# pw2 begins with eight outputs per tile, LayerNorm all on VectorE, and the borders of the stages rewritten

## The chip, the cores and the metric

The kernel runs on all 8 cores of one Trainium2 chip. The metric is device time in microseconds of the slowest core, as the median of several executions. The cores share no data: each works through the whole two-layer network for its own 1024 frames of the prompt (with 160 frames of history in front) and for two of the sixteen short sample sequences of 16 frames. So a microsecond that leaves the longest chain of one core leaves the time.

## The reference, cut to what matters

Everything is kept transposed, with channels on the 128 partitions (2048 channels are 16 chunks, called c or n) and frames along the free axis. Layer 0 mixes with a convolution module and layer 1 with sliding-window attention; each is followed by a SwiGLU. D is 2048, D_FF 5632.

```python
def conv_module(h, state, ...):
    a, gt = split(h @ w_pw1 + b_pw1, 2)
    u = a * sigmoid(gt)
    z = depthwise_conv(concat(state, u), width 31) + b_dw
    z = silu(layer_norm(z, ln_g, ln_b))        # per frame, over 2048 channels
    return z @ w_pw2 + b_pw2, last 30 frames of u

h = modulate(rms_norm(x, norm_mix), sh1, sc1)  # both layers
x = x + g1 * mixer(h)                          # conv_module, then attention
h = modulate(rms_norm(x, norm_ffn), sh2, sc2)
x = x + g2 * ((silu(h @ w_g) * (h @ w_u)) @ w_down)
...
y = rms_norm(x, norm_out)
```

Results are the normalized frames, the last 30 inputs of the convolution, and the keys and values of the newest 128 frames. All products run in bf16 with fp32 accumulation.

## The kernel before, in words

A core's columns stand in three tiles: columns 0 to 383, 384 to 767 and 768 to 1183 (widths 384, 384, 416; in layer 1 from wo on the first is 256 wide). The last tile holds 32 sample columns, whose modulation has another scale, so its evictions come in three pieces. Every engine's program is written out by hand: a helper `wait` puts semaphore waits ahead of the next instruction, and nothing is reordered afterwards. `mm` (line 229) issues every matmul, `act` (line 232) every ScalarE instruction and `dma` (line 224) every transfer, which is why most rows carry these three lines.

**Weights** go through RING, nine slots of 2048 columns. A block of 16 chunks takes two slots, a block of 8 takes one. `ring_use` makes TensorE wait for a block, `ring_release` marks it free once TensorE has finished, and `ring_fill` then issues the next loads in the fixed order of `plan`, on GpSimd's queue. A load can be issued only when the blocks that lie in its slots have been released.

**From the convolution to pw2.** `shift_copies` lays four shifted copies of a chunk of u, with 16 VectorE copies; `conv_tile` runs the depthwise convolution as small matmuls, ScalarE evicts z and its square, and VectorE adds both up in ACCZ and ACC2. `stat_sums` sums these over the partitions with fp32 matmuls, and `stat_factors` makes mean and 1/std of a tile. `ln_apply(t, c)` normalizes chunk c of tile t: subtract the mean (three chunks of four on GpSimd, one of four on VectorE, lines 928 and 931), multiply by 1/std (VectorE, line 933), silu on ScalarE into ZS; then SP reloads x into the place of z. pw2 has 16 output chunks. Six of them (three blocks of weights) are accumulated while the rows of a tile come, chunk by chunk in six banks, tile after tile. The six evictions of a tile (`epilogue_bias`: ScalarE into one of two buffers TMP2, then VectorE adds to x, line 456) stand behind the first rows of the next tile in ScalarE's program. The other ten outputs follow in `pw2_group`, one output of one tile at a time, in banks 3 to 6; block 3 is loaded while the six are at work, since three blocks hold six of the nine slots.

**Norms.** A `Norm` squares each finished output on ScalarE (four buffers), and TensorE adds the square to the sum of its tile in bank t; this add is put off by two groups of matmuls (`late`). When a tile has its sixteen adds, ScalarE makes 1/rms (Ln and Exp, another function table than Silu), and sixteen `scale` steps go to a list `behind`, which `after_group` empties by a credit of time: VectorE multiplies by 1/rms, ScalarE scales and shifts into HB. `samples` (lines 556 to 562) does the sample columns of the last tile and stands behind its sixteen rows. `need` empties the list up to the tile that TensorE is about to read. The last norm writes its result with `final`: four chunks on VectorE into one of two buffers, then a transfer to memory.

**SwiGLU.** For each of six groups G, `gate_up` makes the products of up to eight blocks and `down` adds their part of the output to x. The first two blocks of a layer are taken together, tile by tile, then the others one at a time. At the end of a stage `tile_outer` takes the last blocks together, so that the first tile is finished first: the last three blocks of pw2, of wo and of layer 0's `down`, and all eight of layer 1's `down`, each in the order of tiles 0, 1, 2.

**Attention** begins with `k_group` and `v_group`; the weights q_6 and q_7 are waited for before the first of them.

## Time and profile before

| | |
|---|---|
| median of 3 executions | 3349.31 us (3344.06 to 3625.43) |
| profiled execution | 3347.12 us |
| its span, slowest core | 3346.0 us |
| all cores' spans | 3325.3 to 3346.0 us |
| mean granted TensorE clock | 0.957 to 0.963 of full speed |
| TensorE busy | 3041.8 us, 91% of the span |
| VectorE / ScalarE / GpSimd busy | 1221.0 / 752.7 / 335.1 us |

The profiled execution's time is its span and 1.1 us around it. TensorE is the engine of the chain that ended last for 81% of the span, so the kernel's time is TensorE's work plus what TensorE waits and what it runs at the lower of its two clock levels (1.2 and 2.4 GHz; the granted clock is given as a share of the higher). The page cuts the span in 40 slices of 83.6 us:

```profile
PE   2399996889999999999999889898999999999996
...
PEclk8599997999999999999999999799999999999998
```

Both lines are full over most of the span. The slices that are not are the start, slices 7 to 9 (from 502 to 753 us: the end of the convolution, LayerNorm, pw2), the ones around 1840 to 1920 us (into attention), around 2090 to 2340 us (out of attention, wo, the next norm), and the last two.

### The profile page before, as it was taken

The numbers are of one execution on the slowest core, as the hardware profiler recorded it, in microseconds if no ns is written. First come the engines' busy times: TensorE is split into PE (matmuls) and PEld (weight loads), VectorE is DVE, ScalarE is ACT, GpSimd is POOL, SyncE is SP. The second block draws the span as 40 slices with busy tenths as digits, with TensorE's granted clock in tenths as the row PEclk, the third lists the DMA queues.
The fourth block names the chain that finished last, engine by engine and source line by source line (L and its number), as shares of the span: only waits on it lengthen the run. The fifth ranks groups of instructions, "written<-read, shape, count | busy, mean of one in ns | idle before, by whom it ended". The sixth has DMA issues, their size and how long they took to land.

```text
span 3346.0 us, 58403 instructions; the slowest of 8 cores (3325.3 to 3346.0 us)
## 1 busy us (share of the span) xinstructions
PE 3041.8 (91%) x23532; PEld 1857.9 (56%) x23566; DVE 1221.0 (36%) x2690; ACT 752.7 (22%) x1743; POOL 335.1 (10%) x510
## 2 busy tenths in 40 slices
PE   2399996889999999999999889898999999999996
PEld 0155553455556565565565555455566666666653
DVE  0356677331321414123413548723131313132315
ACT  1412224571000000000002647646100000000012
POOL 0000005000000000000001035410000000000000
PEclk8599997999999999999999999799999999999998
DMA  9977774525757475674667123032674444343432
GB/s 218 150 113 126 128 127 90 118 51 101 127 99 133 75 134 104 110 130 76 109 126 120 23 55 58 18 70 51 115 127 75 76 73 79 64 80 54 84 61 104
DMA packets 73592, 320.57 MB, mean 96 GB/s; under 512 B 11952, under 2 KB 28176, under 8 KB 45808
## 3 DMA queue, kind: packets, MB, share of 16 engines
q0 software_dynamic: 49440, 283.78, 48.9%
q1 hardware_dynamic: 23888, 33.06, 3.3%
q8 instruction: 192, 3.15, 0.4%
q14 instruction: 72, 0.59, 0.1%
HBM read 590.55 MB, written 10.70 MB: 180 GB/s over the span
## 4 chain that ended last, share of the span: by engine, by line
PE 81%; DVE 5%; ACT 5%; DMA 4%; issue 3%; another core or an unknown queue 1%; SPq 0%; DVEq 0%; ACTq 0%; POOL 0%; POOLq 0%
PE ps L229 80%; ACT SCR L232 2%; DMA RING<-wmod 2%; ACT HBraw L232 1%; DMA X<-xT 1%; PE ps L1349 1%; DVE X L933 1%; DMA RING<-wpw 1%; ACT RING L232 1%; DVE X L465 1%; DVE UBraw L578 1%; DVE UBraw L1355 1%; DVE X L456 0%; SPq L224 0%
## 5 line engine op out<-in xcount | busy, mean ns | idle before, releaser
L229 PE MATMUL ps<-HBraw,RING 128*128 128x384 bf16 (+4 forms) x10816 | 1762.4, 325 | 35.8 <-DVE HBraw L562 15.0
L229 PEld LDWEIGHTS ps<-HBraw,RING 128*128 128x128 bf16 x10848 | 1050.2, 98 | 716.1 <-issue 56.3
L229 PE MATMUL ps<-UBraw,RING 128*128 128x384 bf16 (+3 forms) x6016 | 968.9, 319 | 41.6 <-ACT SCR L232 22.1
L229 PEld LDWEIGHTS ps<-UBraw,RING 128*128 128x128 bf16 x6016 | 571.4, 99 | 403.9 <-issue 78.7
L620 DVE TENSOR_TENSOR UBraw<-ps,SCR 128x384 bf16<-128x384 f32 (+2 forms) x264 | 144.4, 547 | 1194.7 <-PE ps L229 1175.7
L232 ACT ACTIVATE SCR<-ps 128x384 f32<-128x384 f32 (+2 forms) x264 | 127.0, 481 | 1787.2 <-PE ps L229 1787.2
L465 DVE SCALAR_TENSOR_TENSOR X<-ps,MOD,X 128x384 f32<-128x384 f32 (+2 forms) x960 | 389.6, 447 | 319.9 <-PE ps L229 318.7
L224 POOL DMA_DIRECT2D RING<-wgu x88 | 46.5, 529 | 1094.6 <-PE ps L229 1091.1
L229 PE MATMUL ps<-SCT,RING 128*128 128x3 bf16 x3072 | 91.3, 165 | 64.3 <-DMA RING<-wmod 54.4
L224 POOL DMA_DIRECT2D RING<-wmod x96 | 51.5, 537 | 877.5 <-PE ps L229 869.1
L229 PEld LDWEIGHTS ps<-SCT,RING 128*128 128x128 bf16 x3072 | 89.8, 97 | 74.9 <-issue 66.8
L232 ACT ACTIVATE RING<-RING,NM 128x193 f32<-128x193 f32 (+1 forms) x264 | 116.7, 444 | 55.0 <-DVE NM L1317 54.9
L794 DVE COPY UBraw<-UBraw 32x1256 bf16<-32x1256 bf16 (+2 forms) x272 | 125.1, 460 | 5.1
L232 ACT ACTIVATE SCR<-X 128x384 bf16<-128x384 f32 (+3 forms) x160 | 88.0, 572 | 158.8 <-DVE X L465 68.3
L229 PE MATMUL ps<-SCR,ONESB 128*128 128x384 bf16 (+6 forms) x206 | 59.8, 349 | 69.5 <-ACT SCR L232 67.2
L229 PE MATMUL ps<-UBraw,SCR 128*32 128x384 bf16 (+4 forms) x2336 | 114.1, 295 | 5.1 <-DVE UBraw L794 3.0
L456 DVE TENSOR_TENSOR X<-X,SCR 128x384 f32<-128x384 f32 (+2 forms) x84 | 47.2, 562 | 180.7 <-ACT SCR L232 180.7
L232 ACT ACTIVATE HBraw<-SCR,MOD,AM 128x384 bf16<-128x384 f32 (+2 forms) x144 | 89.5, 689 | 44.0 <-DVE MOD L398 35.1
L224 POOL DMA_DIRECT2D RING<-wdn x96 | 50.9, 540 | 462.3 <-PE ps L229 462.0
L232 ACT ACTIVATE SCR<-ps,VTs 128x512 f32<-128x512 f32 (+5 forms) x116 | 63.4, 566 | 141.8 <-PE ps L229 141.6
L229 PEld LDWEIGHTS ps<-UBraw,SCR 128*32 128x32 bf16 (+2 forms) x2336 | 64.3, 98 | 48.3 <-issue 12.4
L767 DVE SCALAR_TENSOR_TENSOR UBraw<-ps,VTs,SCR 128x512 bf16<-128x512 f32 (+4 forms) x112 | 39.7, 402 | 115.6 <-ACT SCR L232 113.6
(95 smaller groups left out, 1235.3 us busy)
## 6 DMA issues: line engine op xcount, KB each, us to landing
RING<-wmod POOLq DMA_DIRECT2D x96, 1024.0 KB, 13.6
RING<-wgu POOLq DMA_DIRECT2D x88, 1024.0 KB, 8.9
RING<-wdn POOLq DMA_DIRECT2D x80, 512.0 KB, 8.2
RING<-wpw POOLq DMA_DIRECT2D x24, 1024.0 KB, 17.0
X<-xT SPq DMA_DIRECT2D x4, 2368.0 KB, 55.6
RING<-wqkv POOLq DMA_DIRECT2D x16, 512.0 KB, 6.5
X<-xT SPq DMA_DIRECT2D x32, 192.0 KB, 2.4
RING<-wo POOLq DMA_DIRECT2D x5, 1024.0 KB, 8.5
```

Of the source, the lines that this page charges most:

```text
L224: engw.e.dma_start(out=out, in_=in_).then_inc(sem, 16)
L229: return PE.emit(nc.tensor.matmul(out, lhsT=lhsT, rhs=rhs, start=start, stop=stop, **kw))
L232: return ACT.emit(nc.scalar.activation(out=out, in_=in_, func=func, **kw))
L456: DVE.emit(nc.vector.tensor_tensor(out=X[:, n, xlo:xlo + zn], in0=X[:, n, xlo:xlo + zn], in1=tmp[:, e, 0:zn], op=ALU.add))
L465: DVE.emit(nc.vector.scalar_tensor_tensor(out=X[:, n, a:b_], in0=PS[bk][:, a - xlo:b_ - xlo], scalar=MOD[:, li, 80 + n, bi:bi + 1], in1=X[ ...
L578: DVE.emit(nc.vector.scalar_tensor_tensor(out=YS[:, i, c % 4, 0:zn], in0=X[:, c, xlo:xlo + zn], scalar=VTs[:, VO["nout"] + c:VO["nout"] + ...
L620: DVE.emit(nc.vector.tensor_tensor(out=ACTR[:, 8 * (G % 2) + j - FIRST[G], xlo:xlo + zn], in0=bu[:, 0:zn], in1=SG[:, p, 0:zn], op=ALU.mult))
L767: DVE.emit(nc.vector.scalar_tensor_tensor(out=out, in0=ba[:, lo:hi], scalar=ba_s, in1=SGC[:, kk % 2, lo:hi], op0=ALU.add, op1=ALU.mult))
L794: DVE.emit(nc.vector.tensor_copy(out=U4[32 * s:32 * s + 32, cb, j, lo:hi], in_=U[32 * j:32 * j + 32, cb, 8 * s + lo:8 * s + hi]))
L933: DVE.emit(nc.vector.tensor_tensor(out=z, in0=z, in1=ACC2[:, zlo:zlo + zn], op=ALU.mult))
L1349: PE.emit(nc.tensor.transpose(PTB[0:hi - lo, c + 128 * u:c + 128 * u + 128], PB[i % 2][:, u, lo:hi], IDB[:]))
L1355: DVE.emit(nc.vector.tensor_copy(out=PTS[0:rows, i % 2, lo:hi], in_=PTB[0:rows, lo:hi]))
```

## The change: what it does

1. **LayerNorm.** `ln_apply` does the subtraction always on VectorE; GpSimd does none. `stat_sums(2)` and `stat_factors(2)` move behind the fourth row of tile 0, and the Ln and Exp of tile 2 (`stat_root`, split off) behind its sixteenth silu.
2. **pw2.** Four blocks are held. For each tile six outputs are accumulated as rows come and two more (n = 6, 7) behind them, from rows that are all there. The evictions of the six stand right behind them, in four buffers (TMP4), ahead of the next tile's rows; those of the two stand behind the fifth row of the next tile. Eight outputs are left for `pw2_group`.
3. **Last convolution chunk.** Four of sixteen shifting copies go to ScalarE, and the taps stand behind the copies.
4. **Norms.** Adds are put off by three groups instead of two; in pw2 and wo a square is issued one group later (`last`); every third `scale` step is done on VectorE alone; `samples` stands ahead of the sixteen rows of the last tile.
5. **SwiGLU.** The first three blocks of a layer are taken together instead of two, and the squares left over are flushed behind the first of their nine products. Layer 1's last `down` does block 0 for all tiles, then the seven others in the order of tiles 2, 1, 0.
6. **Attention.** q_6 and q_7 are waited for just ahead of their own products.

```diff
+        TMP4 = carve(SCR, 17152, (128, 4, 416), F32)
...
-                late.append((pe_groups[0] + 2, lambda: self.add(t, i, ta)))
+                late.append((pe_groups[0] + 3, lambda: self.add(t, i, ta)))
...
+                    if t == 2:
+                        behind.append((1.5, t, lambda: self.samples(tr)))
                     for c in range(KC):
                         behind.append((0.62, t, lambda c=c: self.scale(t, c, tr)))
-                    if t == 2:
-                        behind.append((1.5, t, lambda: self.samples(tr)))
...
-                ACT.wait(DVE.tick())
-                act(HB[:, c, 32 + xlo:32 + xlo + zn], self.tmp[:, i, 0:zn], AF.Identity, scale=AM[:, c, 0:1],
-                    bias=MOD[:, self.li, self.sh0 + c, 0:1])
-                self.tfree[i] = ACT.tick()
+                am, sh, row = AM[:, c, 0:1], MOD[:, self.li, self.sh0 + c, 0:1], HB[:, c, 32 + xlo:32 + xlo + zn]
+                if c % 3 == 2:
+                    DVE.wait(DVE.tick())
+                    DVE.emit(nc.vector.tensor_scalar(out=row, in0=self.tmp[:, i, 0:zn], scalar1=am, scalar2=sh,
+                                                     op0=ALU.mult, op1=ALU.add))
+                    self.tfree[i] = DVE.tick()
+                else:
+                    ACT.wait(DVE.tick())
+                    act(row, self.tmp[:, i, 0:zn], AF.Identity, scale=am, bias=sh)
...
                 if G == 0:
-                    two = [ring_use(f"gu{li}_{j}") for j in js[:2]]
+                    some = {}
                     for t in range(3):
-                        for j in (0, 1):
-                            gate_up(two[j][0], j, t, G)
+                        for j in js[:3]:
+                            if t == 0:
+                                some[j] = ring_use(f"gu{li}_{j}")
+                            gate_up(some[j][0], j, t, G)
+                            if t == 0 and j == js[0]:
+
+                                flush_late()
                             if t == 2:
-                                ring_release(two[j][1])
-                    js = js[2:]
+                                ring_release(some[j][1])
+                    js = js[3:]
                     flush_late()
...
-                inner = 5 if after.out else 0
+                inner = 5 if after.out else 1
                 for b in range(inner):
                     slot, bi = ring_use(f"dn{li}_{G}_{b}")
                     for n in (2 * b, 2 * b + 1):
                         for t in range(3):
                             down(slot, n, t, G)
                     ring_release(bi)
-                tile_outer([ring_use(f"dn{li}_{G}_{b}") + (2 * b,) for b in range(inner, 8)], tiles,
-                           lambda slot, n, t: down(slot, n, t, G))
+                tile_outer([ring_use(f"dn{li}_{G}_{b}") + (2 * b,) for b in range(inner, 8)],
+                           lambda slot, n, t: down(slot, n, t, G), (0, 1, 2) if after.out else (2, 1, 0))
             yield
 
...
+        def shift_copies(c, lo, hi, both=False):
+
             cb = c % 2
+            if both:
+                ACT.wait(DVE.tick(), conv_t[c - 2, 2])
             for j in range(4):
                 for s in range(4):
-                    DVE.emit(nc.vector.tensor_copy(out=U4[32 * s:32 * s + 32, cb, j, lo:hi],
-                                                   in_=U[32 * j:32 * j + 32, cb, 8 * s + lo:8 * s + hi]))
+                    out, in_ = U4[32 * s:32 * s + 32, cb, j, lo:hi], U[32 * j:32 * j + 32, cb, 8 * s + lo:8 * s + hi]
+                    if both and s == 3:
+                        act(out, in_, AF.Copy)
+                    else:
+                        DVE.emit(nc.vector.tensor_copy(out=out, in_=in_))
 
         def taps(c):
             DVE.emit(nc.vector.tensor_tensor(out=DG[:, c % 2, :, :], in0=M4[:].unsqueeze(1).to_broadcast([128, 32, 32]),
...
-            POOL.wait(rs_t[t])
             DVE.wait(rs_t[t])
-            if c % 4:
-                POOL.emit(nc.gpsimd.tensor_tensor(out=z, in0=z, in1=ACCZ[:, zlo:zlo + zn], op=ALU.subtract))
-                DVE.wait(POOL.tick())
-            else:
-                DVE.emit(nc.vector.tensor_tensor(out=z, in0=z, in1=ACCZ[:, zlo:zlo + zn], op=ALU.subtract))
-                DVE.wait(DVE.tick())
+            DVE.emit(nc.vector.tensor_tensor(out=z, in0=z, in1=ACCZ[:, zlo:zlo + zn], op=ALU.subtract))
+            DVE.wait(DVE.tick())
...
-        blocks = [ring_use(f"pw2_{b}") for b in range(3)]
-        waiting = []
-        pk = 2
-        for t, (zlo, zn) in enumerate(L0T):
-            now = [(pk + n) % 8 for n in range(6)]
-            pk += 6
-            for c in range(KC):
-                ln_apply(t, c)
-                if t == 0 and c == 3:
-                    stat_factors(2)
-                if c < len(waiting):
-                    ready.append((waiting[c][1], t - 1, pw2_out(*waiting[c])))
+            return n, t, epilogue_bias(0, n, zlo, zn, bk, tp, xr_t[t, n // 4], TMP4)
+
+
+
+        blocks = [ring_use(f"pw2_{b}") for b in range(4)]
+        six = (4, 5, 6, 7, 2, 3)
+
+        def pw2_mm(t, n, bk, c):
+            zlo, zn = L0T[t]
+            mm(PS[bk][:, 0:zn], blocks[n // 2][0][:, c, 128 * (n % 2):128 * (n % 2) + 128], ZS[:, c, zlo:zlo + zn],
+               c == 0, c == KC - 1)
+
+        for c in range(4):
+            ln_apply(0, c)
+        for t in range(3):
             for c in range(KC):
                 PE.wait(ap_t[t, c])
                 for n in range(6):
                     if c == 0:
-                        PE.wait(bfree[now[n]])
-                    mm(PS[now[n]][:, 0:zn], blocks[n // 2][0][:, c, 128 * (n % 2):128 * (n % 2) + 128],
-                       ZS[:, c, zlo:zlo + zn], c == 0, c == KC - 1)
-                    if c == KC - 1:
-                        now[n] = (t, n, now[n], PE.tick())
-            waiting = now
-        for slot, bi in blocks:
-            ring_release(bi)
-        for args in waiting:
-            ready.append((args[1], 2, pw2_out(*args)))
+                        PE.wait(bfree[six[n]])
+                    pw2_mm(t, n, six[n], c)
+                if t == 0 and c == 3:
+                    stat_sums(2)
+                    stat_factors(2)
+                    for c2 in range(4, KC):
+                        ln_apply(0, c2)
+                    stat_root(2)
+            tp = PE.tick()
+            for n in range(6):
+                ready.append(pw2_out(t, n, six[n], tp))
+            if t == 2:
+                for slot, bi in blocks[:3]:
+                    ring_release(bi)
+            two = []
+            for n in (6, 7):
+                PE.wait(bfree[n - 6])
+                for c in range(KC):
+                    pw2_mm(t, n, n - 6, c)
+                two.append((t, n, n - 6, PE.tick()))
+            if t < 2:
+                for c in range(5):
+                    ln_apply(t + 1, c)
+            for args in two:
+                ready.append(pw2_out(*args))
+            if t < 2:
+                for c in range(5, KC):
+                    ln_apply(t + 1, c)
+        ring_release(blocks[3][1])
...
-            norm1.square(n, t, pw2_out(t, n, bk, PE.tick()))
-            if ready:
-                norm1.square(*ready.popleft())
+            if last:
+                norm1.square(*last.popleft())
+            last.append(pw2_out(t, n, bk, PE.tick()))
+            for _ in range(2 if n < 10 else 1):
+                if ready:
+                    norm1.square(*ready.popleft())
             after_group(1.3)
...
-        q3 = [use_halves("q_6"), use_halves("q_7")]
+        q3 = []
...
+                if t == 0 and n % 2 == 0:
+                    q3.append(use_halves(f"q_{n // 2}"))
...
-            norm3.square(n, t, epilogue_bias(1, n, xlo, zn, bk, PE.tick()))
+            if last:
+                norm3.square(*last.popleft())
+            last.append((n, t, epilogue_bias(1, n, xlo, zn, bk, PE.tick())))
```

How the instructions stand now, at the three places that the prediction speaks of. First TensorE's program from the last convolution chunk into pw2, before the change (`UBraw,SCR` are convolution matmuls, `SCR,ONESF` the sums of `stat_sums`, `UBraw,RING` pw2, `SCR,ONESB` the adds of squares):

```order
L229 MATMUL ps<-UBraw,SCR 32x384 x32
L229 MATMUL ps<-UBraw,SCR 32x32 x32
L229 MATMUL ps<-SCR,ONESF 128x384 x2
L229 MATMUL ps<-SCR,ONESF 128x416 x2
L229 MATMUL ps<-UBraw,RING 128x384 x192
L229 MATMUL ps<-UBraw,RING 128x416 x96
L229 MATMUL ps<-UBraw,RING 128x384 x32
L229 MATMUL ps<-SCR,ONESB 128x384 x2
L229 MATMUL ps<-UBraw,RING 128x416 x16
L229 MATMUL ps<-SCR,ONESB 128x384 x2
L229 MATMUL ps<-UBraw,RING 128x384 x16
```

And in the changed program:

```order
L230 MATMUL ps<-UBraw,SCR 32x384 x32
L230 MATMUL ps<-UBraw,SCR 32x32 x32
L230 MATMUL ps<-SCR,ONESF 128x384 x2
L230 MATMUL ps<-UBraw,RING 128x384 x24
L230 MATMUL ps<-SCR,ONESF 128x416 x2
L230 MATMUL ps<-UBraw,RING 128x384 x232
L230 MATMUL ps<-UBraw,RING 128x416 x128
L230 MATMUL ps<-UBraw,RING 128x384 x32
L230 MATMUL ps<-SCR,ONESB 128x384
L230 MATMUL ps<-UBraw,RING 128x416 x16
L230 MATMUL ps<-SCR,ONESB 128x384 x3
```

The sums of tile 2 moved behind the first four rows of pw2 (24 matmuls), and 384 instead of 288 matmuls of pw2 stand ahead of the first add of a square.

ScalarE's program through the rows, before (`UBraw<-X,VTs` is a silu, `SCR<-ps,G1B,MOD` an eviction of pw2, the pair with `EPSC` the Ln and Exp of a tile):

```order
L232 ACTIVATE SCR<-SCR,EPSC 128x384
L232 ACTIVATE SCR<-SCR 128x384
L232 ACTIVATE UBraw<-X,VTs 128x384 x4
L232 ACTIVATE SCR<-SCR,EPSC 128x416
L232 ACTIVATE SCR<-SCR 128x416
L232 ACTIVATE UBraw<-X,VTs 128x384 x13
L232 ACTIVATE SCR<-ps,G1B,MOD 128x384
L232 ACTIVATE UBraw<-X,VTs 128x384
L232 ACTIVATE SCR<-ps,G1B,MOD 128x384
L232 ACTIVATE UBraw<-X,VTs 128x384
```

And in the changed program:

```order
L233 ACTIVATE SCR<-SCR,EPSC 128x384
L233 ACTIVATE SCR<-SCR 128x384
L233 ACTIVATE UBraw<-X,VTs 128x384 x16
L233 ACTIVATE SCR<-SCR,EPSC 128x416
L233 ACTIVATE SCR<-SCR 128x416
L233 ACTIVATE SCR<-ps,G1B,MOD 128x384 x6
L233 ACTIVATE UBraw<-X,VTs 128x384 x5
L233 ACTIVATE SCR<-ps,G1B,MOD 128x384 x2
L233 ACTIVATE UBraw<-X,VTs 128x384 x11
L233 ACTIVATE SCR<-ps,G1B,MOD 128x384 x6
L233 ACTIVATE UBraw<-X,VTs 128x416 x5
L233 ACTIVATE SCR<-ps,G1B,MOD 128x384 x2
```

The six evictions of a tile no longer alternate with silus of the next, and the Ln and Exp of tile 2 stand between tile 0's last silu and tile 0's evictions.

TensorE's program from the last pw2 groups into the SwiGLU of layer 0 (`HBraw,RING`), before:

```order
L229 MATMUL ps<-UBraw,RING 128x416 x16
L229 MATMUL ps<-SCR,ONESB 128x416
L229 MATMUL ps<-HBraw,RING 128x384 x32
L229 MATMUL ps<-SCR,ONESB 128x416
L229 MATMUL ps<-HBraw,RING 128x384 x96
L229 MATMUL ps<-HBraw,RING 128x416 x64
L229 MATMUL ps<-HBraw,RING 128x384 x64
L229 MATMUL ps<-HBraw,RING 128x416 x32
```

And in the changed program:

```order
L230 MATMUL ps<-UBraw,RING 128x416 x16
L230 MATMUL ps<-SCR,ONESB 128x416
L230 MATMUL ps<-HBraw,RING 128x384 x32
L230 MATMUL ps<-SCR,ONESB 128x416 x3
L230 MATMUL ps<-HBraw,RING 128x384 x160
L230 MATMUL ps<-HBraw,RING 128x416 x96
L230 MATMUL ps<-HBraw,RING 128x384 x64
L230 MATMUL ps<-HBraw,RING 128x416 x32
```

The left-over squares of tile 2 stand behind the first product, and five products (160 matmuls) instead of three stand between them and the first that reads tile 2 (128x416).

## Rows read from the trace of the kernel before

**Rows 1.** The page: its first line.

```profile
span 3346.0 us, 58403 instructions; the slowest of 8 cores (3325.3 to 3346.0 us)
```

**Rows 2.** Stretches: length, busy PE, PEld, DVE, ACT, POOL, clock, DMA share, GB/s.

```profile
538.00:630.00 92.00, 59.78 (x290) 29.39 (x288) 61.13 (x81) 51.81 (x85) 41.85 (x36) 0.82 0.39 109
630.00:793.00 163.00, 146.07 (x878) 82.35 (x879) 48.75 (x94) 87.04 (x163) 4.76 (x9) 0.95 0.35 64
1785.00:1925.00 140.00, 126.65 (x768) 74.42 (x767) 68.39 (x165) 70.81 (x130) 7.51 (x14) 0.98 0.34 56
2205.00:2377.00 172.00, 150.30 (x1189) 97.86 (x1188) 48.83 (x100) 87.55 (x179) 5.81 (x11) 0.97 0.39 71
3230.00:3331.00 101.00, 77.58 (x448) 43.45 (x446) 46.42 (x114) 28.65 (x56) 0.53 (x1) 0.94 0.18 58
```

**Rows 3.** Timeline of TensorE at the borders: start, length, instructions, idle before.

```profile
760.49 30.39 PE L229 MATMUL ps<-HBraw,RING 128*128 128x416 bf16 x160 [7.48 <-DVE HBraw L562]
...
1854.56 0.32 PE L229 MATMUL ps<-UBraw,ONESB 128*128 128x384 bf16 x1 [4.55 <-ACT UBraw L232]
...
1875.19 4.44 PE L229 MATMUL ps<-HBraw,RING 128*128 128x384 bf16 x16 [3.11 <-DMA RING<-wqkv]
...
2347.89 28.58 PE L229 MATMUL ps<-HBraw,RING 128*128 128x416 bf16 x160 [7.47 <-DVE HBraw L562]
...
3238.40 3.24 PE L229 MATMUL ps<-UBraw,RING 128*128 128x256 bf16 x16 [5.68 <-DMA RING<-wdn]
```

**Rows 4.** The same view, VectorE and GpSimd, end of convolution and LayerNorm.

```profile
509.24 6.88 DVE L794 COPY UBraw<-UBraw 32x1000 bf16<-32x1000 bf16 x16
...
539.48 4.97 DVE L933 TENSOR_TENSOR X<-X,SCR 128x384 f32<-128x384 f32 x4
...
587.23 0.55 DVE L931 TENSOR_TENSOR X<-X,SCR 128x384 f32<-128x384 f32 x1
587.88 1.97 DVE L933 TENSOR_TENSOR X<-X,SCR 128x384 f32<-128x384 f32 x4
...
533.04 45.17 POOL L928 TENSOR_TENSOR X<-X,SCR 128x384 f32<-128x384 f32 x36 [13.45 <-ACT SCR L232]
626.05 1.63 POOL L224 DMA_DIRECT2D RING<-wpw  x3 [47.83 <-issue]
```

**Rows 5.** The same view, TensorE in pw2.

```profile
542.97 6.55 PE L229 MATMUL ps<-UBraw,RING 128*128 128x384 bf16 x24 [3.83 <-ACT UBraw L232]
...
580.14 18.15 PE L229 MATMUL ps<-UBraw,RING 128*128 128x384 bf16 x94 [3.21 <-ACT SCR L232]
...
630.06 6.98 PE L229 MATMUL ps<-UBraw,RING 128*128 128x384 bf16 x32 [5.91 <-ACT SCR L232]
...
640.34 2.76 PE L229 MATMUL ps<-UBraw,RING 128*128 128x384 bf16 x16
642.94 0.73 PE L229 MATMUL ps<-SCR,ONESB 128*128 128x416 bf16 x2
```

**Rows 6.** The same view, ScalarE in LayerNorm.

```profile
549.12 1.28 ACT L232 ACT_TABLE_LOAD   x1
550.42 2.50 ACT L232 ACTIVATE UBraw<-X,VTs 128x384 bf16<-128x384 f32 x4
...
568.27 0.65 ACT L232 ACTIVATE SCR<-ps,G1B,MOD 128x384 f32<-128x384 f32 x1
...
623.37 6.54 ACT L232 ACTIVATE SCR<-ps,G1B,MOD 128x384 f32<-128x384 f32 x18 [3.79 <-PE ps L229]
```

**Rows 7.** The loads of weights issued in 624:628, in the view of RING.

```profile
DMA to landing us min/median/max: 11.8/16.9/21.3
```

**Rows 8.** Stretches view of 2110:2150, in attention.

```profile
2110.00:2150.00 40.00, 27.38 (x217) 15.49 (x214) 30.23 (x51) 28.46 (x115) 21.08 (x26) 0.53 0.19 35
```

**Rows 9.** Timeline of VectorE at the end.

```profile
3330.98 4.59 DVE L578 SCALAR_TENSOR_TENSOR UBraw<-X,VTs,SCR 128x416 f32<-128x416 f32 x8 [2.69 <-ACT SCR L232]
3337.30 4.74 DVE L578 SCALAR_TENSOR_TENSOR UBraw<-X,VTs,SCR 128x416 f32<-128x416 f32 x8 [1.73 <-DMA yT<-UBraw]
```

More of the change, by code:

```diff
@@ L583, in final, with tile_outer @@
                                   YS[:, i, :, 0:zn], yst_sem[i])
-        def tile_outer(blocks, tiles, body):
-            for t in range(3):
+        def tile_outer(blocks, body, order=(0, 1, 2)):
+            for t in order:
                 for slot, bi, n0 in blocks:
@@ L740, in build_nc @@
         u4_t = {}
+        u4a_t = []
         conv_t = {}
@@ L903, in stat_factors @@
             rs_t[t] = ACT.tick()
-        PE.wait(u4_t[KC - 1])
+        PE.wait(u4_t[KC - 1], *u4a_t)
+        set_gb("bpw2", 0, 32)
         for b in range(2):
@@ L1444, in build_nc @@
         pk = 0
+        last = deque()
         def wo_group(rows, n, t):
@@ L1470, in build_nc @@
                 ring_release(i)
-        tile_outer([ring_use(f"wo_{b}") + (2 * b,) for b in (5, 6, 7)], L1T,
+        tile_outer([ring_use(f"wo_{b}") + (2 * b,) for b in (5, 6, 7)],
                    lambda slot, n, t: wo_group(whole(slot), n, t))
+        norm3.square(*last.popleft())
         DVE.wait(kv_t[0], kv_t[1])
```

39 lines of the change are left out of this document (21 added, 18 removed).

## The prediction

> **What bounds the kernel now.** I read the page first: TensorE is busy for 91% of a span of 3346.0 us [rows 1], so what can be won is TensorE's waits and its time at 1.2 GHz. The slices with low clock lie at borders of stages; the view of stretches gives each its size [rows 2]. From 538 to 630 us TensorE is busy 59.8 of 92.0 us at a granted clock of 0.82; in the four other stretches it idles 16.9, 13.4, 21.7 and 23.4 us (length minus busy). The timeline names the longest waits at these borders [rows 3]: for the sample columns of the last tile (7.48 and 7.47 us), for a burst on ScalarE when a tile's norm is made (4.55), for q_6 and q_7 (3.11) and for a block of `down` (5.68). After such a wait TensorE runs at the lower level: 16 matmuls of 384 columns take 4.44 us behind the wait of 3.11 [rows 3], where at 2.4 GHz they are 2.60 us from start to start (640.34 to 642.94) [rows 5], 0.1625 each; 416 columns are then 0.173.
>
> **LayerNorm and pw2 (changes 1 to 3).** On VectorE four multiplications take 1.97 us when GpSimd is silent, 0.49 each, and 4.97, 1.24 each, inside GpSimd's run of 45.17 us [rows 4]. Without GpSimd a row costs its subtraction, 0.65 from start to start (587.23 to 587.88), and 0.49: 1.14 us, or 1.20 at 416 columns. TensorE needs 6 x 0.1625 = 0.98 for it, so VectorE sets the pace.
>
> Start: 12 instead of 16 copies save 4 x 0.43 = 1.7 us [rows 4] and the shorter ones another 0.9 by their columns. No row shows the copies on ScalarE. Four of 1000 columns are at least 4 x 0.62 (a 384-column silu [rows 6]), at most 1000/384 times that, 2.5 to 6.5 us; VectorE's share (5.2, and about 1.2 for the taps) covers them, save for a few tenths at the top. I take 2.6 us for this, and 2.8 us for accumulation and factors that GpSimd no longer slows. The first row starts at 542.97 - 5.4 = 537.6.
>
> Tile 0: four rows as now, 6.5 us [rows 5]. Then comes a new wait: the moved sums (2.5 us, my estimate between 1.7 and 3.1), the factors on VectorE (2.0, three operations in sequence), one row (1.1) and its silu (0.7), and TensorE idles some 4 us before the fifth row at 550.5; it starts at 551.27 now. Eleven rows, the matmuls of the last and some slow ones give 564.5 for the six outputs. The pair behind needs 32 x 0.1625 = 5.2 us and covers part of the next interval.
>
> Intervals: six evictions at 0.65 on ScalarE [rows 6], the last addition 0.6, sixteen rows 18.2, the two evictions behind the fifth row 2.5 (VectorE waits for silus and evictions), last silu 0.7, its matmuls 1.0: 26.9 us; 28.1 at 416 columns. Between tiles 0 and 1 the Ln and Exp of tile 2 add 2.8, as each switch of table is 1.28 [rows 6]. So the six of tile 1 end at 594.2, of tile 2 at 622.3, the pair at 627.9. SP's reloads of x, one behind each silu, come closer together, but the evictions need rows 0 to 7 only, asked for 8 rows earlier: nothing. In the trace the table load of 549.12 is followed by a silu at 550.42 [rows 6], so a switch costs the load alone. The Trainium skill ("ScalarE: Activation LUTs", What ACT_TABLE_LOAD costs) gives 1283 ns plus a drain of about 1380 ns for each. By that the two switches would make the interval 2.8 us longer; the trace shows no such drain, and the sum leaves it out.
>
> Then the weights. The plan needs pw2_0's slots for pw2_4, and with four blocks held (eight of nine slots) nothing is loaded ahead. The release falls at 622.3. Of three loads issued together at 626.05 [rows 4] the first landed after 11.8 us, the others after 16.9 and 21.3 [rows 7]. I take 11.8, the same position in the same queue: TensorE waits until 634.1, 6.2 us, and loses 1.4 in the restart as at 630.06 now (6.98 for 32 [rows 5], 5.2 at full rate). With an idle memory it could be 9; with more in flight, 16.9, and both stay in the range. At 635.5, 24 of 48 output tiles are done. Now 18 are done at 630.06, and six more with their adds take 20.1 (3.1 each, 1.4 slow): 650.2. **Term A: 14.7 us.**
>
> **Into the SwiGLU (changes 4, 5).** From 630 to 793 us TensorE idles 16.9 and loses 4.7 at the low level (1.4 after a burst; 3.3 after 760.49, where 160 matmuls take 30.39 [rows 3] against about 27.1). Nine products stand at the head instead of six before another block, five instead of three ahead of tile 2, and the samples come first: the wait of 7.48 and its restart go. Putting adds off by one more group and one square later covers most of the bursts, but four square buffers bound it. A third of the rows goes to VectorE: 45 in three norms at 0.5 us, 22 us; it is busy 48.8 of 163 us here [rows 2], so they hide behind TensorE. No row shows this form; half of it or twice it hides too, unless several stand together. I leave 4.5 us of waits and 2 for adds that no longer fall in the first six groups. **Term B: 15.5 us** (8 to 19).
>
> **Into attention (4, 6).** 13.4 idle and 3.2 at the low level. The wait for q_7 moves behind the first products of k and v, by when it has landed; but the last rows of tile 0's norm were made behind it and are late next, about 1.5 us. I leave 7. **Term C: 9.5** (5 to 12).
>
> **wo into the SwiGLU (4, 5).** 21.7 idle, 3.4 slow after 2347.89; 2.5 of it is a barrier that stays, 5.5 I leave: **term D: 17** (11 to 20). The third block held was requested two groups of wo before the stage and is needed after two products, some 14 us later.
>
> **The end (5).** 23.4 idle and 4 slow. Block 0 gives 8.6 us of work while block 7 loads (5.68 of waiting goes). The last tile is 256 wide, so its `final` steps are shorter; now they are two runs of 4.59 and 4.74 us with a store between them [rows 9]. Of the idle time about 9 stays, the bursts; the tail behind the last matmul shrinks by some 3.5. **Term E: 22** (13 to 27).
>
> Sum: 14.7 + 15.5 + 9.5 + 17 + 22 = 78.7. The profiled execution took 3347.12; minus 78.7 it is 3268.4. The median of the runs stands 2.2 above the profiled execution, which gives 3270.6: **3271 us**, 2.3% less.
>
> **The rivals.**
>
> *Bursts stay.* The adds may be held by the four buffers whatever the delay, and evictions queue behind Ln, Exp and scaled rows as now. For it: waits up to 4.55 us [rows 3] are longer than one group of `down` (1.6). Against: the long waits for samples and loads do not depend on it. B, C, D and E lose about 5 each: 3291.
>
> *The low clock stays in pw2.* A row leaves TensorE 0.16 us idle in 1.14, and each tile begins with a wait. In attention the clock stood at 0.53 for 40 us with TensorE busy 27.4 of them [rows 8]. Against: at 1.2 GHz a row needs 1.95 us and TensorE would be busy without a gap; at 580.14, 94 matmuls took 18.15 us [rows 5], 2.9 over the full rate, so it had returned. If half of the 63 us of row work runs slow, 30 us are lost, part of it hidden: 3296. The Trainium skill ("TensorE: Matmul & The Clock Gate", A second HAM failure mode: psum-queue depth-cycling) tells of a kernel whose short idles between groups made the clock go back and forth. That is this rival's mechanism; no row here shows it for gaps of 0.16 us.
>
> *Slower than before.* The same clock, kept from the first row to the last of the nine products, 537 to 757 us. That is 63 (384 matmuls), 70 (24 outputs with 36 adds) and 48 (nine products), 181 us of work at full rate; each of it at 1.2 GHz costs as much again. It decides from 79 us of such work on, where the sum is used up; all of it gives 3271 + 181 = 3452. Against it: between 640 and 690 us the groups ran at 2.60 with adds between them.
>
> *It does less than it says*: LayerNorm waits for reloads of x or the queue of SP, and A is nothing: 3286.
>
> *More than the sum*: bursts vanish and the block lands early, 20 us: 3251.
>
> **How the numbers follow.** A measurement of this kernel can tell about 2% from no change, that is 3282 us. Forecast as summed: 0.55, with its own range 3256 to 3286, of which 0.49 under 3282. More: 0.10. Bursts stay: 0.15. Low clock in pw2: 0.10, half of it with other terms at their low ends. A is nothing: 0.07. Slower: 0.03. Faster by over 2% is then 0.59, same 0.38, slower 0.03. The lower end takes in the case with more, the upper all low ends together with a late block: 78.7 less 36: 3307. The range is 3248 to 3308.
>
> **What would show it.** On VectorE single multiplications near 0.5 us all through LayerNorm, and rows 1.14 apart; TensorE with four waits in pw2: behind the fourth row, 3 to 4 us after tile 0, about 1.4 after tile 1, and 6 for RING<-wpw. No wait for DVE HBraw (the samples), none for RING<-wqkv before the first k product, none for RING<-wdn at the end; the tail behind the last matmul near 14 us. I am wrong if pw2's matmuls keep taking 0.32 us, if the wait for pw2_4 passes 10 us, or if a product waits for the third block of a SwiGLU.

## The result, and the profile after

The changed kernel took 3302.99 us (median of four runs, 3299.62 to 3308.97). The ratio to the kernel before is 0.9871, with an interval of 0.9843 to 0.9900: 43 us less, and 32 us more than the 3271 forecast. (Some executions of every kernel, here and below, were disturbed; ratios and the times quoted leave them out, and where few were left the interval is wide.) The mean of the eight cores' spans, which one late core hardly moves, fell from 3335.9 us in the profiled execution to 3291.0, and stands between 3288.8 and 3292.2 in all four runs; some differences below are given in it too. The page is that of core 5, the slowest of the profiled execution:

```profile
span 3300.6 us, 58445 instructions; the slowest of 8 cores (3281.4 to 3300.6 us)
```

All rows that follow are of core 2 unless said otherwise, the core of [rows 1 to 9]; its span fell from 3346.0 to 3292.7, by 53.3 us. To see where they came from I took from the timelines of TensorE the start of each stage's first matmul, on all eight cores, and the time from one such start to the next. Each number is the median of eight cores, in us; the sum is without what lies ahead of pw2 and behind the last matmul. The last row adds up the medians above it; "last gate_up" is its last matmul. The last five columns are experiments of the next section: banks is number 1, halves 5, both 10, delay 2 is 11, old entries 3.

| from ... to | before | after | banks | halves | both | delay 2 | old entries |
|---|---|---|---|---|---|---|---|
| pw2 to first gate_up of SwiGLU 0 | 188.1 | 171.1 | 176.0 | 167.2 | 167.0 | 169.0 | 179.7 |
| to its first down | 146.8 | **159.8** | 149.0 | 142.7 | 141.5 | 141.4 | 150.0 |
| to the last group of down | 904.3 | 904.7 | 904.6 | 904.3 | 904.3 | 904.3 | 904.5 |
| to the first v product | 97.0 | 85.6 | 86.4 | 87.4 | 88.9 | 94.1 | 94.1 |
| attention | 307.0 | 307.8 | 307.0 | 308.2 | 308.8 | 308.4 | 305.2 |
| to first gate_up of SwiGLU 1 | 125.9 | 113.6 | 113.6 | 113.6 | 113.6 | 113.7 | 126.9 |
| to its first down | 136.5 | **148.5** | 145.0 | 135.1 | 132.0 | 130.2 | 135.9 |
| to the last gate_up | 776.9 | 776.8 | 776.9 | 776.8 | 776.9 | 776.8 | 776.9 |
| to the last matmul | 96.8 | 74.8 | 75.0 | 75.0 | 75.1 | 88.8 | 89.4 |
| sum | 2779.2 | 2742.7 | 2733.5 | 2710.3 | 2708.0 | 2726.8 | 2762.6 |

Three stages are 11 to 22 us shorter, pw2 is 17 shorter, and two have become longer: each SwiGLU's stretch up to its first down, by 13.0 and 12.0 us. What wo won (12.3) is gone within 20 us. The view of stretches (length, busy time of each engine with the number of instructions, granted clock, DMA's share, GB/s), for LayerNorm with pw2's first part, the rest of pw2, and the two bad stretches:

```profile
536.00:633.00 97.00, 77.72 (x395) 39.70 (x396) 62.88 (x119) 54.95 (x92) 2.12 (x4) 0.90 0.48 118
633.00:709.00 76.00, 73.06 (x427) 41.61 (x426) 21.78 (x42) 46.37 (x94) 1.59 (x3) 0.98 0.40 75
709.00:869.00 160.00, 140.93 (x1024) 83.41 (x1023) 39.50 (x86) 35.26 (x62) 9.57 (x19) 0.93 0.57 98
2279.00:2428.00 149.00, 128.06 (x1029) 84.59 (x1027) 37.40 (x84) 33.91 (x60) 9.83 (x19) 0.92 0.60 105
```

In the third and fourth TensorE is idle for 19.1 and 20.9 us. The timeline of TensorE says where (start, length, instruction, and in brackets the idle time and who ended it), at the head of SwiGLU 0 and of SwiGLU 1:

```profile
708.64 5.36 PE L230 MATMUL ps<-HBraw,RING 128*128 128x384 bf16 x32
713.84 0.34 PE L230 MATMUL ps<-SCR,ONESB 128*128 128x416 bf16 x1
717.05 0.34 PE L230 MATMUL ps<-SCR,ONESB 128*128 128x416 bf16 x1 [2.88 <-ACT SCR L233]
720.52 0.51 PE L230 MATMUL ps<-SCR,ONESB 128*128 128x416 bf16 x1 [3.13 <-ACT SCR L233]
730.84 61.01 PE L230 MATMUL ps<-HBraw,RING 128*128 128x384 bf16 x352 [9.81 <-ACT SCR L233]
...
2285.41 0.34 PE L230 MATMUL ps<-SCR,ONESB 128*128 128x416 bf16 x1 [2.84 <-ACT SCR L233]
2288.88 0.51 PE L230 MATMUL ps<-SCR,ONESB 128*128 128x416 bf16 x1 [3.13 <-ACT SCR L233]
2298.95 21.27 PE L230 MATMUL ps<-HBraw,RING 128*128 128x256 bf16 x133 [9.57 <-ACT SCR L233]
```

After one product (32 matmuls from HBraw) TensorE does the three adds that the flush issues, waits 6.0 us for their squares and then 9.81 for ScalarE, 15.8 in all, and 15.5 in SwiGLU 1. Before, this place had one wait of 0.85, and the samples 7.48 later [rows 3]:

```profile
737.25 15.76 PE L229 MATMUL ps<-HBraw,RING 128*128 128x384 bf16 x96 [0.85 <-ACT SCR L232]
```

The samples' wait is gone, as intended; the waits of 15.8 and 15.5 us are new. ScalarE in the same stretch (`SCR<-X` is a square, `SCR<-ps,G1B,MOD` an eviction, `HBraw<-SCR,MOD,AM` ScalarE's half of a scaled row, `SCR<-ps` a silu, `SCR<-ps,EPSC` the Ln of a tile's norm):

```profile
708.23 1.16 ACT L233 ACTIVATE SCR<-ps,G1B,MOD 128x384 f32<-128x384 f32 x3
710.64 1.30 ACT L233 ACTIVATE HBraw<-SCR,MOD,AM 128x384 bf16<-128x384 f32 x2 [1.26 <-DVE SCR L544]
711.86 0.53 ACT L233 ACTIVATE SCR<-X 128x416 bf16<-128x416 f32 x1
712.30 1.16 ACT L233 ACTIVATE SCR<-ps,G1B,MOD 128x384 f32<-128x384 f32 x3
715.76 0.71 ACT L233 ACTIVATE HBraw<-SCR,MOD,AM 128x384 bf16<-128x384 f32 x1 [2.31 <-DVE SCR L544]
716.38 0.53 ACT L233 ACTIVATE SCR<-X 128x416 bf16<-128x416 f32 x1
716.82 1.16 ACT L233 ACTIVATE SCR<-ps,G1B,MOD 128x384 f32<-128x384 f32 x3
...
719.84 0.53 ACT L233 ACTIVATE SCR<-X 128x416 bf16<-128x416 f32 x1
720.76 1.31 ACT L233 ACTIVATE HBraw<-SCR,MOD,AM 128x384 bf16<-128x384 f32 x2 [0.38 <-DVE SCR L544]
...
723.47 1.28 ACT L233 ACT_TABLE_LOAD   x1
724.77 0.49 ACT L233 ACTIVATE SCR<-ps 128x384 f32<-128x384 f32 x1
726.54 0.71 ACT L233 ACTIVATE HBraw<-SCR,MOD,AM 128x384 bf16<-128x384 f32 x1 [1.29 <-DVE SCR L544]
728.07 0.71 ACT L233 ACTIVATE HBraw<-SCR,MOD,AM 128x384 bf16<-128x384 f32 x1 [0.82 <-DVE SCR L544]
728.79 1.28 ACT L233 ACT_TABLE_LOAD   x1
730.09 0.61 ACT L233 ACTIVATE SCR<-ps,EPSC 128x416 f32<-128x416 f32 x1
```

Read it from below. The row at 730.09 is tile 2's Ln: it frees bank 2, where the squares were summed, and the second product's banks are 2 and 3, so that TensorE goes on at 730.84. The last square (719.84) has long been added. Between them stand rows, the first product's silu (724.77) and two table loads, because ScalarE works in the order of its program. From above: at each group ScalarE stands idle for 1.26 or 2.31 us, waiting for VectorE's multiplication (L544), with square and eviction queued behind it. Evictions begin at 708.23, 712.30 and 716.82: 4.07 and 4.52 us to a group, where a group takes TensorE 2.97. So ScalarE falls behind. In the kernel before it stood otherwise (its ScalarE, same place):

```profile
726.31 0.55 ACT L232 ACTIVATE SCR<-X 128x416 bf16<-128x416 f32 x1 [0.79 <-DVE X L456]
726.78 1.31 ACT L232 ACTIVATE HBraw<-SCR,MOD,AM 128x384 bf16<-128x384 f32 x2
727.99 1.15 ACT L232 ACTIVATE SCR<-ps,G1B,MOD 128x384 f32<-128x384 f32 x3
```

Eviction, square, rows: the square waited 0.79 for VectorE's addition, and under the square VectorE made the multiplications, so the rows waited for nothing. Put off by one group (change 4), the square comes ahead of the eviction, and the row meets VectorE while it still adds and multiplies. This is read from the rows; no experiment puts the square back alone. What the experiments test is the cure.

### The profile page after: what moved, and what is told of

It reads as the page before. It is cut to its first block, busy times and chain, and to the rows that moved or that the text cites. A ratio compares the mean times of both kernels' runs of the same rounds, so it can differ in the third digit from the quotient of the medians.

```text
span 3300.6 us, 58445 instructions; the slowest of 8 cores (3281.4 to 3300.6 us)
## 1 busy us (share of the span) xinstructions
PE 3030.2 (92%) x23566; PEld 1862.0 (56%) x23566; DVE 1234.4 (37%) x2763; ACT 738.3 (22%) x1710; POOL 290.2 (9%) x474
## 4 chain that ended last, share of the span: by engine, by line
PE 82%; DMA 6%; DVE 5%; ACT 3%; issue 3%; another core or an unknown queue 1%; SPq 0%; DVEq 0%; ACTq 0%; POOL 0%; POOLq 0%
PE ps L230 81%; DMA RING<-wmod 2%; ACT SCR L233 2%; DMA X<-xT 1%; DMA RING<-wgu 1%; DMA RING<-wpw 1%; PE ps L1394 1%; ACT RING L233 1%; DVE SCR L544 1%; ACT HBraw L233 1%; DVE UBraw L1400 0%; DVE X L457 0%; SPq L225 0%; DVE X L952 0%
## 5 line engine op out<-in xcount | busy, mean ns | idle before, releaser
L233 ACT ACTIVATE SCR<-X 128x416 bf16<-128x416 f32 (+3 forms) x160 | 89.8, 571 | 126.4 <-DVE X L466 49.3
L233 ACT ACTIVATE HBraw<-SCR,MOD,AM 128x384 bf16<-128x384 f32 (+3 forms) x114 | 73.9, 696 | 85.7 <-DVE SCR L544 52.8
## 6 DMA issues: line engine op xcount, KB each, us to landing
RING<-wpw POOLq DMA_DIRECT2D x24, 1024.0 KB, 16.5
```

Of the source, the lines that this page charges most:

```text
L233: return ACT.emit(nc.scalar.activation(out=out, in_=in_, func=func, **kw))
```

## The experiments

**1. Other banks.**

```diff
-bg, bu = PS[2 * p], PS[2 * p + 1]
+f = 2 * p + (4 if G == 0 and j < 3 else 0)
+bg, bu = PS[f], PS[f + 1]
...
-                            if t == 0 and j == js[0]:
-                                flush_late()
```

> The first nine products of each SwiGLU use banks 4 to 7 instead of 0 to 3, and the flush of waiting adds behind the first product is gone; the rest is the changed kernel. Theory 'one bank': the second product waits for bank 2, which tile 2's sum of squares holds until its Ln, and the flush puts that Ln on ScalarE behind the first silu, rows and two table loads. TensorE then idles 15.8 us behind the first product of SwiGLU 0 (2.88 + 3.13 + 9.81) and 15.5 behind that of SwiGLU 1. With other banks 10 to 14 us of each go: about 3278 us, ratio near 0.980. Rival 'ScalarE is the bound': evictions, squares and rows that wait for VectorE need this time on ScalarE wherever the adds stand; a product or an add behind waits instead and under 5 us go in all: 3298 to 3303.

Measured: ratio 0.9826 (0.9798 to 0.9854), 3288.4 to 3291.5 us. Between the two: 13 to 15 us gone by median and ratio (10 in the mean of the eight cores), not 25. In the table the stretch behind the first gate_up gets 10.8 us shorter, but the one ahead of it 4.9 longer, and SwiGLU 1 wins 3.5 only. The trace shows the wait in a new place, ahead of the first product:

```profile
702.21 7.40 PE L230 MATMUL ps<-HBraw,RING 128*128 128x384 bf16 x32 [4.80 <-ACT SCR L233]
...
723.84 12.03 PE L230 MATMUL ps<-HBraw,RING 128*128 128x384 bf16 x64 [3.30 <-DVE UBraw L628]
```

Its bank waits for an eviction of pw2, on the same late ScalarE. Both theories hold a part.

**2. The Ln ahead of the first silu.**

```diff
                 tpu = PE.tick()
+                if G == 0 and t == 0 and j == 0:
+                    flush_late()
                 after_group(2.0)
...
-                            if t == 0 and j == js[0]:
-
-                                flush_late()
```

> The flush stays before the second product, but stands ahead of the first silu instead of behind it, so ScalarE makes Ln and Exp of tile 2 first. Theory 'one bank': the waits for the three adds (6.0 us) stay, the third wait (9.81 us) falls to about 1: 17 us in both SwiGLUs, about 3286 us, ratio 0.982. Rival 'ScalarE is the bound': the silu comes later by what the Ln comes earlier, and a product behind waits for it: under 5 us in all, 3298 to 3303.

Measured: ratio 0.9826 (0.9757 to 0.9894), 3288.6 and 3291.0 us: 13 us gone (12 in the mean of the eight cores). That is nearer to 17 than to under 5, but the interval takes in both. Whether the three adds wait as before is not shown.

**3. Old entries** (change 4 and the three blocks of 5 undone; of its edits two are shown).

```diff
-late.append((pe_groups[0] + 3, ...
+late.append((pe_groups[0] + 2, ...
-            if last:
-                norm1.square(*last.popleft())
-            last.append(pw2_out(t, n, bk, PE.tick()))
+            norm1.square(*pw2_out(t, n, bk, PE.tick()))
```

> The changed kernel with changes 4 and 5 undone at all borders: adds put off by two groups and not by one square, samples last, all rows on ScalarE, two blocks held at the head of a SwiGLU and no flush behind the first product. LayerNorm, pw2, the late q_6 and q_7 and the end stay new. Theory 'one bank': what put-off adds and three blocks save is given back at the flush; SwiGLU 0 comes out 4 us earlier, SwiGLU 1 equal, the entry into attention 5 later: 3300 to 3308 us, ratio within 0.002 of the changed kernel's 0.987. Rival 'the entries do save what was forecast and the loss is elsewhere': this kernel is 25 to 30 us slower than the changed one, ratio near 0.996.

Measured: ratio 0.9936 (0.9901 to 0.9971), 3317.1 to 3322.0 us and once 3351.7, slower than the changed kernel by 16 us in the median, 22 by the ratio and 19 in the mean of the eight cores: between the two, and neither had the place. By the table the entries into the SwiGLUs come out near what was expected: pw2 to first down 329.7 for 330.9 (1.2 us less, 4 forecast), wo to first down 262.8 for 262.1. Into attention it is 94.1 for 85.6, 8.5 more where 5 was expected. The rest is the end, whose new order is kept and which takes 89.4 for 74.8: there the delay matters most.

**4. Rows on ScalarE** (`c % 3 == 2` never holds).

> The changed kernel with the third of the norm's rows that went to VectorE put back on ScalarE. Theory 'one bank': ScalarE's queue sets how late the last squares are at both SwiGLUs; 5 rows more per norm tile at 0.65 us make the waits for adds 2 to 4 us longer at each: 3306 to 3312 us. Rival 'the rows on VectorE hold up the additions that the squares need': faster, 3296 to 3300.

Measured: ratio 0.9848 (0.9765 to 0.9931), 3291.8, 3293.3 and 3300.9 us: the rival. Against the changed kernel's 0.9871 the intervals overlap, but the stages add up to 2737.5 for 2742.7, and the mean of the eight cores' spans is 3283.0 to 3283.9 in the three runs, for 3288.8 to 3292.2: 7 us less. A row on VectorE spares ScalarE 0.65 us and costs it a longer wait, 2.31 for 1.26.

**5. Halves apart.** Experiment 1, and ScalarE's half of a row issued one row later:

```diff
-                    ACT.wait(DVE.tick())
-                    act(row, self.tmp[:, i, 0:zn], AF.Identity, scale=am, bias=sh)
-                    self.tfree[i] = ACT.tick()
+                self.half.append(second)      # second(): the same three lines, with this row's tick
+                if len(self.half) > 1:
+                    self.half.popleft()()
```

> The kernel with other banks, and in a norm's rows ScalarE's half of a row is issued one row later than VectorE's multiplication, so that ScalarE has it ready. Theory 'squares first': with the square put one group off, ScalarE goes from the evictions straight to a row and waits 1.26 to 2.31 us for VectorE (addition, then multiplication); a group at the stages' ends takes ScalarE 4.35 us where TensorE needs 2.97. Issued apart, the wait goes, ScalarE needs about 2.9 per group, and the adds are no longer late: from pw2's first matmul to the first down matmul 325.0 becomes 315 to 318 us, wo to first down of SwiGLU 1 258.6 becomes 250 to 252: about 3274 us, ratio 0.978. Rival 'ScalarE's work': its own instructions are what is too long; under 4 us in all, 3287 to 3291.

Measured: 3270.2, 3270.4 and 3271.1 us, ratio 0.9751 (0.9616 to 0.9885). TensorE (core 0, where pw2 begins within 3 us of core 2's in the changed kernel):

```profile
704.14 5.36 PE L230 MATMUL ps<-HBraw,RING 128*128 128x384 bf16 x32 [0.22 <-ACT SCR L233]
709.34 0.52 PE L230 MATMUL ps<-SCR,ONESB 128*128 128x416 bf16 x2
709.69 5.36 PE L230 MATMUL ps<-HBraw,RING 128*128 128x384 bf16 x32
714.89 0.34 PE L230 MATMUL ps<-SCR,ONESB 128*128 128x416 bf16 x1
715.06 5.36 PE L230 MATMUL ps<-HBraw,RING 128*128 128x384 bf16 x32
722.01 18.22 PE L230 MATMUL ps<-HBraw,RING 128*128 128x384 bf16 x110 [1.58 <-DVE UBraw L640]
```

and ScalarE just ahead of it:

```profile
699.36 1.16 ACT L233 ACTIVATE SCR<-ps,G1B,MOD 128x384 f32<-128x384 f32 x3
700.41 0.70 ACT L233 ACTIVATE HBraw<-SCR,MOD,AM 128x384 bf16<-128x384 f32 x1
701.78 0.71 ACT L233 ACTIVATE HBraw<-SCR,MOD,AM 128x384 bf16<-128x384 f32 x1 [0.67 <-DVE SCR L547]
702.39 0.53 ACT L233 ACTIVATE SCR<-X 128x416 bf16<-128x416 f32 x1
702.83 1.16 ACT L233 ACTIVATE SCR<-ps,G1B,MOD 128x384 f32<-128x384 f32 x3
```

The adds wait for nothing, the 15.8 us have become 0.22 and 1.58, and evictions begin 3.47 us apart, with 0.67 of waiting; the six evictions from 690.23 to 705.59 are 3.07 apart on average. From pw2 to the first down it is 309.9 us, less than the 315 forecast, and 248.7 from wo on. The work is the same: it was the waiting inside ScalarE's queue.

**6. The same with all rows on ScalarE.**

> As the kernel with halves apart, and all rows back on ScalarE. Theory 'squares first': VectorE's own rows cost 0.5 us and one more wait each (2.31 instead of 1.26) only while ScalarE waits for VectorE; issued apart they relieve ScalarE, so this is the same or 1 to 3 us slower than the kernel with halves apart. Rival 'VectorE's rows are wrong in any case': 3 to 6 us faster than it.

Measured: 3276.0, 3276.2 and 3276.3 us, ratio 0.9767 (0.9676 to 0.9858). That is 5 to 6 us slower than experiment 5 on the same chip, with three times of each that lie within 1 us, so VectorE's rows help once nobody waits, more than the 1 to 3 expected; in the mean of the eight cores it is 3258.2 against 3264.0, 6 us too. By stages the rows on VectorE win 8.6 from pw2 to the first down and 3.4 from wo on, and cost 2.9 on the way into attention. With experiment 4 this shows that their worth has changed its sign with the order of the queue.

**7. Four pairs of banks**, on top of 6: `f = (0, 4, 6, 2)[(gk[0] - 1) % 4]` in the first nine products.

> As the kernel with halves apart and all rows on ScalarE, and the first nine products use four pairs of banks in turn (0, 4, 6, 2). Theory 'banks': the first product no longer waits 4.8 us for an eviction of pw2's last groups, the fourth not 3.3 for VectorE: 5 to 8 us less in both SwiGLUs together. Rival: the waits are for the adds' squares and move there, under 2 us.

Measured: 3265.9, 3266.7 and 3268.0 us, ratio 0.9739 (0.9648 to 0.9830): 9.5 us less than experiment 6, and 7.8 in the mean of the eight cores, at the upper end of the forecast.

**8. Changes 1 to 3 alone**, on the kernel before.

> The kernel before with the changes up to the end of pw2 alone (copies, LayerNorm on VectorE, eight outputs, sums). Forecast as on record: term A, 14.7 us, about 3332 to 3336 us, ratio 0.9956. By the stage table of the changed kernel 12 to 16 us. A rival is that the gain is lost again at the entry of SwiGLU 0, where a block's load or the samples set the time: under 5 us, ratio over 0.998.

Measured: ratio 0.9945 (0.9906 to 0.9984), 3330.2 to 3336.5 us where the kernel before took 3342.6 to 3343.7 in four of six runs beside it: about 10 us, or 13.5 in the mean of the eight cores (3321.7 for 3335.2 in those four). The first is a little under term A, the second close to it. By the table's count pw2 to first gate_up is 180.0 for 188.1, the next stretch 148.7 for 146.8, the end 95.9 for 96.8; what the earlier start of pw2 brings lies ahead of these.

**9. Halves apart alone**, with the old banks and the flush.

> The changed kernel with one edit: ScalarE's half of a norm's row is issued one row later than VectorE's multiplication; banks and the flush behind the first product stay. Theory 'squares first': the wait for VectorE between evictions and row is what makes the squares late, so the waits for three adds at the flush (2.88 and 3.13 us of them) go and the Ln behind them comes 6 us earlier; of 330.9 us from pw2's first matmul to the first down matmul 10 to 14 go, of 262.1 from attention to the first down of SwiGLU 1 7 to 10: 3278 to 3286 us, ratio 0.980 to 0.982. Rival 'the bank is needed too, and first': without other banks less than 8 us go in all: over 3294.

Measured: ratio 0.9813 (0.9796 to 0.9830), 3277.1 to 3283.5 us: within the forecast; this one edit wins about 20 us beyond the changed kernel's 43. From pw2 to the first down it takes 317.5 us for 330.9, from wo to the first down 251.3 for 262.1. What is left is the bank, alone now:

```profile
711.69 0.69 PE L230 MATMUL ps<-SCR,ONESB 128*128 128x416 bf16 x3
719.44 15.79 PE L230 MATMUL ps<-HBraw,RING 128*128 128x384 bf16 x86 [7.07 <-ACT SCR L233]
```

The three adds run without a pause, and 7.07 us are waited for the Ln. So the two causes add up, late squares and the Ln in the queue: at the first border the banks alone win 5.9 us, the halves alone 13.4, both together 21.0; at the second 3.5, 10.8 and 13.4.

**10 and 12. Both, with a third of the rows on VectorE** (experiment 5 with the four pairs of 7).

> Halves apart, a third of the rows on VectorE, and the first nine products on four pairs of banks (0, 4, 6, 2). Both theories: the best of the kernels so far. From the kernel with halves apart and two pairs, 1 to 4 us less at the entries, since the first product finds a free bank: 3266 to 3270 us, ratio near 0.974.

> The kernel with both once more, for its ratio: its stages in the profiled execution, from pw2's first matmul on, are 2.3 us shorter together than those of the kernel with halves apart and two pairs of banks. Theory: banks and halves act each for itself, 3264 to 3270 us, ratio 0.973 to 0.978. Rival: what four pairs save at the head of SwiGLU 1 is taken back by the loads behind it, and the ratio is over 0.979.

Measured: the first gave 3267.7 us in its profiled execution and no ratio; the second a ratio of 0.9734 (0.9680 to 0.9787), at best 3264.7 us. This is the best kernel here, by 0.9734 against 0.9871 about 1.4% faster than the changed one; its interval overlaps those of experiments 5 and 7, and in the mean of the eight cores it is 3.7 and 1.7 us under them (3254.6 against 3258.2 and 3256.3).

**11. A delay of two groups**, in the kernel of experiment 10.

> As the kernel with both, but an add falls due two groups after its square instead of three. Theory 'delay': at the end, where a group of down takes 1.6 us and one square with its eviction and addition takes longer than two groups, the third group is what covers the burst; the stage from the last gate_up to the last matmul goes from 75 to 86 to 90 us, the rest stays: about 12 us more, ratio near 0.978. Rival 'not the delay but the squares put off and three blocks': under 3 us.

Measured: 3284.4 us in the profiled execution, and no ratio. By the stages of its eight cores the end takes 88.8 for 75.1 and the entry into attention 94.1 for 88.9; wo stays at 113.7 for 113.6, where old entries had 126.9. It is one execution, but alike on eight cores: the third group covers bursts where groups are short (down). Neither the delay nor the rows on VectorE (113.8 in experiment 4) changes wo, so the square put off, the only other edit that acts there, is what shortens it. The view of waits for the end (3200 us to the end), of the changed kernel and of this one (total, times, longest):

```profile
PE ps L230 <- ACT SCR L233: 7.7, 5, 3.3
```

```profile
PE ps L230 <- ACT SCR L233: 14.4, 11, 4.4
```

## Why the prediction was wrong

Core 2 by the prediction's own terms (from starts of its timeline, before and after):

| term | forecast | measured | from |
|---|---|---|---|
| A, to 24 of 48 output tiles | 14.7 | 16.7 | 650.2, now 631.00 + 7.72 - 5.2 = 633.5 |
| B, to the first down | 15.5 | **-5.3** | first down 880.5, now 869.1: 11.4, less 16.7 |
| C, down to v | 9.5 | 12.9 | 97.5, now 84.6 |
| attention | 0 | 4.3 | 311.2, now 306.9; other cores from 3 us shorter to 5 longer |
| D, wo to the first down | 17 | **-0.1** | 262.5, now 262.6 |
| E, the end | 22 | 25.2 | 96.8, now 73.5, and the tail 16.5, now 14.6 |

These sum to 53.7; the span moved by 53.3. The slowest cores moved by 45.4 (3346.0 to 3300.6), because core 2 was the slowest before, having begun pw2 last of all (543.0), and now core 5 is: it begins 1.2 us behind core 2 (537.5 against 536.3), takes 2.9 more to the first v product and 3.3 more in attention.

That 3303 us lies inside the stated range of 3248 to 3308 is owed to its width: B and D each came out far below their own ranges (8 to 19, 11 to 20).

**A was right**, and step by step:

```profile
536.35 5.97 PE L230 MATMUL ps<-UBraw,RING 128*128 128x384 bf16 x24 [8.94 <-ACT UBraw L233]
...
547.88 18.79 PE L230 MATMUL ps<-UBraw,RING 128*128 128x384 bf16 x104 [4.17 <-ACT UBraw L233]
570.17 6.71 PE L230 MATMUL ps<-UBraw,RING 128*128 128x384 bf16 x30 [3.50 <-ACT UBraw L233]
...
596.02 6.01 PE L230 MATMUL ps<-UBraw,RING 128*128 128x416 bf16 x30 [1.21 <-ACT UBraw L233]
604.62 19.17 PE L230 MATMUL ps<-UBraw,RING 128*128 128x416 bf16 x98 [2.59 <-ACT UBraw L233]
631.00 7.72 PE L230 MATMUL ps<-UBraw,RING 128*128 128x384 bf16 x32 [7.21 <-DMA RING<-wpw]
```

First row 536.35 (537.6 forecast), fifth 547.88 behind 4.17 us (550.5, some 4), 3.50 after tile 0 (3 to 4), 1.21 after tile 1 (1.4), 7.21 for pw2_4 (6.2), and a slower restart behind it (7.72 for 32 matmuls, 2.5 over the full rate, for 1.4). The wait of 2.59 behind tile 2's fifth row is the 2.5 that the forecast had for the two evictions there. VectorE's rows stand 1.14 apart:

```profile
578.37 0.55 DVE L950 TENSOR_TENSOR X<-X,SCR 128x384 f32<-128x384 f32 x1
579.03 0.56 DVE L952 TENSOR_TENSOR X<-X,SCR 128x384 f32<-128x384 f32 x1
579.51 0.55 DVE L950 TENSOR_TENSOR X<-X,SCR 128x384 f32<-128x384 f32 x1
```

The granted clock was 0.90 over this stretch (0.82 before [rows 2]), and 1.00 in the row work from 576 to 586 us, so the low clock as a rival fell too. What the Trainium skill says of short idles between groups ("TensorE: Matmul & The Clock Gate", A second HAM failure mode: psum-queue depth-cycling) was not seen for a row's 0.16 us. Nor was the drain behind a table load, about 1380 ns in the Trainium skill ("ScalarE: Activation LUTs", What ACT_TABLE_LOAD costs): the load at 723.47 takes 1.28 and the silu follows at 724.77. **C and E were right in their sums**, and the rows of tile 0 that C had late by 1.5 us cost 0.67 + 0.28 + 0.88 between 1852 and 1856. But E names only block 0's 5.68 us and leaves open what takes the other waits away: experiments 3 and 8 give the new order 6.5 us (95.9 to 89.4), and the delay of three 13 to 15 (experiments 3 and 11).

**B and D failed**, in the same sentence, which is the step of the prediction that was wrong: "putting adds off by one more group and one square later covers most of the bursts". It holds where no product is near that needs the squares' bank and no row stands in ScalarE's queue. I had counted VectorE's 22 us as hidden "unless several stand together", and ScalarE's queue not at all. Two things were to be read before. In the code, the flush stands behind the first product for a reason: the second product takes bank 2, so three adds, an Ln and all that is queued ahead of it come between two products. In the trace, ScalarE's wait of 0.79 for VectorE covered the rows' multiplications; whoever moves the square moves this cover. Of the rivals "bursts stay" named evictions queued behind rows, but priced a border at 5 us; 20.8 and 17.1 were lost at two, and nothing at the others, so its 3291 is not a forecast of what happened.

The saving itself was there. With the halves apart and other banks (experiment 5), pw2 to the first down takes 309.9 us where experiment 8, with changes 1 to 3 only, takes 328.7: 18.8 us for B's 15.5. From wo to the first down it is 248.7 for 262.4 before, and 245.6 with four pairs of banks: 13.7 and 16.8 for D's 17. The best kernel stands at 3266.7 us (median), near the forecast 3271, but by two edits of which the forecast knew nothing.

What stays open: whether experiment 2's Ln ahead of the silu gains more or less than the other banks of experiment 1 (both 0.9826); whether the put-off square alone, put back, would also end the late squares; and why attention is 4.3 us shorter on core 2 and 3.2 on core 4, unchanged on core 6 and up to 5.3 longer on the others (over eight cores of one kernel it differs by up to 6.5 us).

## What to carry to other kernels

When work is put off to cover a wait, ask on each in-order queue what it now stands ahead of, and find the first later instruction that needs its bank or buffer: a flush there turns the delay into a stall. Between two engines that hand a row back and forth, issue the second half one step later: this alone won about 20 us. Take one engine's wait in a trace as possible cover for another's work, and compare stages start to start on all cores: a median over eight showed 12 us lost at a border within a kernel that was 43 us faster.
